# A two-block model step on one core: the end of the state-space branch and the last attention written in another order

## The reference

```python
def mamba2_branch(z, xbc, dt_raw, ...):
    xbc = silu(causal_dwconv(xbc, conv_w) + conv_b)
    xs, bm, cm = split(xbc)                       # 2048, 512, 512 channels
    dt = softplus(dt_raw + dt_bias)               # 32 heads of 64 channels, 4 groups
    y = ssd_chunked(xs, dt, -exp(a_log), bm, cm)  # per head: (cb * decay) @ (dt * x)
    y = y + d_skip[:, None] * xs                  # the D term
    yg = y * silu(z)                              # then a norm over each group of 512 channels
    yg = yg * rsqrt(mean(yg * yg, axis=-1, keepdims=True) + EPS)
    return (yg * norm_g) @ w_out

def sliding_window_attention(q, k, v, sinks):     # 12 query heads of 64, 2 key heads
    s = einsum(q, k) * 64 ** -0.5                 # masked to the band
    m = maximum(max(s), sink)
    p = exp(s - m); p = p / (sum(p) + exp(sink - m))
    return einsum(p, v)                           # rotary positions are applied to q and k before
```

## Time and profile before

| | us |
|---|---|
| median of 3 runs | 1700.3 (1697.75 to 1701.42) |
| profiled execution, own time | 1702.51 |
| its span | 1700.7 |
| z stage, transposes and cb, gate_b | 405.9 to 481.5 |
| y groups between mem_k and mem_v | 497.6 to 566.9 |
| group norm sums to the start of ssm_out | 566.9 to 588.4 |
| ssm_out, mix | 588.4 to about 660 |
| last attention, then wo1 | 1414.8 to 1474.3, from 1474.3 |

### The profile page before, as it was taken

How to read it: one execution, slowest core, us unless ns; L and a number is a source line. 1 busy time by engine, 2 the same in 40 slices (tenths; PEclk the granted TensorE clock), 3 DMA queues, 4 the chain that set the end, 5 groups by cost and what they waited for, 6 DMA issues and landing times.

```text
span 1700.7 us, 21777 instructions
## 1 busy us (share of the span) xinstructions
PE 1584.5 (93%) x8746; PEld 1357.5 (80%) x8746; DVE 583.1 (34%) x1040; ACT 807.3 (47%) x1192; POOL 1166.0 (69%) x490
## 2 busy tenths in 40 slices
PE   4999999999978698999999999889999988899997
PEld 3888879999967577878878888877888876578886
DVE  4111018245449712331121586552113046521100
ACT  4444363466353435355454773135444353355443
POOL 4888868887756286478877872606887952078883
PEclk9999999999989898999999998989999987899998
DMA  6555645555545154355545542004555631055551
GB/s 210 173 192 192 204 167 185 187 184 194 164 140 175 54 178 137 102 198 183 189 161 193 192 155 78 1 25 136 195 176 198 195 123 55 25 174 182 189 197 51
DMA packets 71861, 259.80 MB, mean 153 GB/s; under 512 B 7984, under 2 KB 8784, under 8 KB 71504
## 3 DMA queue, kind: packets, MB, share of 16 engines
q1 hardware_dynamic: 68832, 249.59, 44.3%
q10 hardware_dynamic: 2928, 8.81, 1.5%
HBM read 257.29 MB, written 1.08 MB: 152 GB/s over the span
## 4 chain that ended last, share of the span: by engine, by line
PE 86%; DVE 7%; ACT 5%; issue 2%; DMA 0%; POOL 0%; ACTq 0%; DVEq 0%
PE bank L459 12%; PE bank L461 12%; PE bank L460 12%; PE bank L429 7%; PE bank L430 7%; PE bank L431 6%; PE bank L488 5%; PE bank L490 5%; PE bank L489 5%; PE bank L568 1%; ACT w_hi L1000 1%; PE bank L614 1%; PE bank L840 1%; PE bank L852 1%; PE bank L637 1%
## 5 line engine op out<-in xcount | busy, mean ns | idle before, releaser
L387 POOL TENSOR_TENSOR w_lo<-raw,w_hi 128x1024 fp32r<-128x1024 f32 x474 | 1143.1, 2433 | 464.6 <-ACT w_hi L1000 464.1
L1000 ACT ACTIVATE w_hi<-raw 128x1024 fp32r<-128x1024 f32 x474 | 489.1, 1057 | 467.1 <-PE bank L461 211.6
L459 PE MATMUL bank<-w_hi,u_hi 128*128 128x512 f32 x880 | 352.1, 400 | 31.5 <-POOL w_lo L387 20.0
L461 PE MATMUL bank<-w_hi,u_lo 128*128 128x512 f32 x880 | 346.2, 393 | 0.0
L460 PE MATMUL bank<-w_lo,u_hi 128*128 128x512 f32 x880 | 346.1, 393 | 0.0
L429 PE MATMUL bank<-u_hi,w_hi 128*128 128x256 f32 x880 | 252.8, 287 | 12.9 <-DVE u_lo L1584 6.4
L430 PE MATMUL bank<-u_lo,w_hi 128*128 128x256 f32 x880 | 250.6, 285 | 0.0
L431 PE MATMUL bank<-u_hi,w_lo 128*128 128x256 f32 x880 | 250.6, 285 | 0.0
L459 PEld LDWEIGHTS bank<-w_hi,u_hi 128*128 128x128 f32 x880 | 167.4, 190 | 68.3 <-issue 22.7
L461 PEld LDWEIGHTS bank<-w_hi,u_lo 128*128 128x128 f32 x880 | 167.3, 190 | 36.0
L460 PEld LDWEIGHTS bank<-w_lo,u_hi 128*128 128x128 f32 x880 | 167.6, 190 | 33.4
(11 more groups left out here) (354 smaller groups left out, 1871.3 us busy)
## 6 DMA issues: line engine op xcount, KB each, us to landing
raw<-in_w SPq DMA_DIRECT2D x474, 512.0 KB, 4.2
bc<-acs_scratch ACTq DMA_DIRECT2D x8, 512.0 KB, 5.8
mem_t<-in_mem ACTq DMA_DIRECT2D x2, 1024.0 KB, 7.7
xf<-in_x ACTq DMA_DIRECT2D x2, 512.0 KB, 8.3
out<-out_t SPq DMA_DIRECT2D x4, 256.0 KB, 2.8
lvl<-in_lvl ACTq DMA_DIRECT2D x1, 448.0 KB, 5.6
band<-in_band ACTq DMA_DIRECT2D x1, 256.0 KB, 5.2
tri<-in_tri ACTq DMA_DIRECT2D x1, 192.0 KB, 7.8
```

Of the source, the lines that this page charges most:

```text
L387: nc.gpsimd.tensor_tensor(w_lo[:, q % RAW, :], raw[:, q % RAW, :], w_hi[:, q % HI, :].bitcast(F32), ALU.subtract).then_inc(split_done, 1)
L459: mm(b[:], hi[:, kt, a], w_hi[:, q % HI:q % HI + 2, c], start=kt == 0, stop=False)
L461: m = mm(b[:], lo[:, kt, a], w_hi[:, q % HI:q % HI + 2, c], start=False, stop=kt == KT - 1)
L1000: fn(w_hi[:, q % HI, :], raw[:, q % RAW, :], ACT.Copy).then_inc(hi_made, 1)
```

## The change

The state-space end is written anew, and so is the last attention; the start is changed a little.

- **dt first.** dt is ahead of xbc; its chain of small steps lies beside the convolution's taps (shares 1, 1, 3, 3, 4 of its steps beside the first five chunks), as do cols and the transposes of x behind chunks 6 to 10.
- **z and y tokens-first.** z is a pair stage. y has the decay tile stationary (128x128) and moves 64 columns of x; the D term is added on TensorE by four matmuls with the identity, of x that VectorE has scaled. Three `dec` buffers instead of two. After gating, the square with a sum along the row (ScalarE), root, reciprocal and scaling make the group norm; the matmuls with ones go. Then y is transposed (`y_turn`), and y_hi, y_lo are made from PSUM with the norm's weights.
- **Order of TensorE** from z on: z, with y groups 0 to 4 between its halves, gate_b with y groups 5 to 7, ssm_out, mem_k, mix, mem_v; the memory norm's squares, root and scaling lie under ssm_out; the merged turns and xattn's turns stand between mem_k and mem_v.
- **Last attention** ("merge and padding"): mq1 first, q1's halves between the heads, wo1's first tiles between the last heads; k, v and the memory's k, v in zero-padded tiles so that every matmul has 128 rows and 128 columns; rotation as two accumulated matmuls; 128 instead of 256 keys for the first query half; normalising on ScalarE; two heads accumulate into one output.
- **Start.** ScalarE and VectorE wait for `par` alone and no longer for ident, ones and tri; ScalarE feeds the first two pieces behind four u_hi steps.

```diff
-    ("xbc", 12, "row"), ("dt", 1, "row"), ("z", 8, "row"), ("gate_b", 4, "pair"),
-    ("mem_k", 4, "row"), ("mem_v", 4, "pair"), ("ssm_out", 8, "acc"), ("mix", 4, "proj"),
+    ("dt", 1, "row"), ("xbc", 12, "row"), ("z", 8, "pair"), ("gate_b", 4, "pair"),
+    ("ssm_out", 8, "acc"), ("mem_k", 4, "row"), ("mix", 4, "proj"), ("mem_v", 4, "pair"),
...
+            def y_heads(hg):
...
+                pe.wait_ge(W["decay"], hg + 1)
+                pe.wait_ge(W["x_d"], hg + 1)
+                for hh in range(4):
...
+                    mm(b0, d[:, hh, 0:P], x_dt[:, g, 0, o], start=first, stop=False, skip_group_check=True)
+                    mm(b1, d[:, hh, P:S], x_dt[:, g, 0, o], start=first, stop=False, skip_group_check=True)
+                    mm(b1, d[:, hh, S:384], x_dt[:, g, 1, o], start=False, stop=False, skip_group_check=True)
+                for t in range(2):
+                    for c in range(2):
...
+                        m = mm(flat(y_bank(g, c))[:, o], xbc[:, 2 * hg + t, c * P:c * P + P], ident[:], start=False,
+                               stop=hg % 2 == 1 and t == 1, skip_group_check=True)
+                m.then_inc(W["y_mm"], 1)
+            def y_turn(g):
+
+                for c in range(2):
+                    pe.wait_ge(W["g_n"], 2 * g + c + 1)
+                    for t in range(4):
+                        m = nc.tensor.transpose(quads(y_bank(g, c))[:, t, :], z[:, c, 512 * g + P * t:512 * g + P * t + P], ident[:])
+                    m.then_inc(W["y_t"], 1)
...
-            for g in range(4):
-                b = start_unit(U0["gn"] + g)
-                pe.wait_ge(W["g_sq"], g + 1)
-                for t in range(4):
-                    m = mm(b[:, 0, :], ones[:], sqg[:, t, :], start=t == 0, stop=t == 3)
...
+            y_heads(0)
+            half("z", 2, 0)
+            y_heads(1)
+            half("z", 2, 1)
+            y_heads(2)
+            y_turn(0)
+            half("z", 3, 0)
+            y_heads(3)
+            half("z", 3, 1)
+            y_heads(4)
+            y_turn(1)
+            half("gate_b", 0, 0)
+            y_heads(5)
+            half("gate_b", 0, 1)
+            y_heads(6)
+            y_turn(2)
+            half("gate_b", 1, 0)
+            y_heads(7)
+            half("gate_b", 1, 1)
+            y_turn(3)
...
+            acc_stage("ssm_out", lambda q: pe.wait_ge(W["y_lo"], 2 * (q // 4) + 2), None, lambda: merged_turn(0),
+                      (8, lambda: mem_sum(0, sq_mem, bank[(G0["mem_k"] + 3) % 4])), 4)
+            row_stage("mem_k", mm_hi, mm_lo, lambda kt: pe.wait_ge(mem_lo, kt // 2 + 1), sub=(0, 1))
+            merged_turn(1)
...
+            after(q0 + 9)
+            after(q0 + 11)
+            evict("z", 2, z, ACT.Silu)
+            decays(3)
+            y_square(0)
+            after(q0 + 13)
+            decays(4)
+            y_hi(0)
...
+                dve.wait_ge(W["seg_exp"], hg + 1)
+                v.tensor_tensor(dec[hg % 3][:], dec[hg % 3][:], cbm[:, hg // 2:hg // 2 + 1, :].to_broadcast([P, 4, 384]), ALU.mult).then_inc(W["decay"], 1)
...
+                if hg >= 2 and hg % 2 == 0:
+                    y_gate(hg // 2 - 1)
+                if hg + 2 < NHG:
+                    seg(hg + 2)
+                if hg >= 3 and hg % 2:
+                    y_norm(hg // 2 - 1)
...
+            row_stage("mq1", u_hi, u_lo)
+            rotate(0)
+            row_stage("q1", u_hi, u_lo, sub=(0, 1))
+            scores(0)
+            scores(1)
+            scores(2)
+            row_stage("q1", u_hi, u_lo, sub=(1, 1), halves=(0,))
+            rotate(1)
+            turns(0)
...
-            act.wait_ge(W["loaded_par"], 64)
+            act.wait_ge(W["loaded_par"], 16)
...
-                if kt in (1, 3):
-                    feed(1 if kt == 1 else 2)
+                if kt == 3:
+                    feed(2)
```

More of the change, by code:

```diff
@@ L969, in _ @@
-            pe.wait_ge(unit_free, _u)
-            proj_stage("wo1", u_hi, u_lo, lambda s, kt: None, lambda: turn("ffn3", 0))
+            rotate(0)
[6 more added lines that the diff above has]
+            turns(0)
+            row_stage("q1", u_hi, u_lo, sub=(1, 1), halves=(1,))
+            turns(1)
+            turns(2)
+            row_stage("q1", u_hi, u_lo, sub=(2, 1), halves=(0,))
@@ new lines, in _ @@
+            rotate(2)
+            heads_out(0)
+            turns(3)
+            turns(4)
+            heads_out(1)
+            row_stage("q1", u_hi, u_lo, sub=(2, 1), halves=(1,))
+            turns(5)
+            turns(6)
+            rotate(3)
+            heads_out(2)
+            turns(7)
+            turns(8)
+            heads_out(3)
+            turns(9)
+            turns(10)
+            heads_out(4)
+            pe.wait_ge(row_free, G0["q1"] + 3)
+            wo1_tiles(6, 7)
+            turns(11)
@@ L971, in _ @@
+            wo1_tiles(0)
+            turns(12)
+            heads_out(5)
+            wo1_tiles(1)
+            turns(13)
+            wo1_tiles(2)
+            turns(14)
+            heads_out(6)
+            wo1_tiles(3)
+            turns(15)
+            heads_out(7)
+            wo1_tiles(4, 5)
+            proj_stage("wo1", h_hi, h_lo, None, lambda: turn("ffn3", 0), pairs=(1,))
             ffn(3, lambda s: turn("ffn3", 1) if s == 0 else None, split_ready("ffn3"))
@@ new lines, in _, with evict @@
+            after(P0["dt"] - 1)
+            act.wait_ge(row_free, G0["dt"] + 1)
+            chain(act, W["row_step"], ROW_STEPS, "alog", lambda: fn(rows[5][0:32, 0:1], col("a_log", 0, 0, 32), ACT.Exp))
+            conv("xbc", "ssm_conv", "ssm_conv_b", xbc, 4, 12, beside)
+            def evict(name, p, dst, what):
+                for s in range(2):
+                    if s:
+                        act.wait_ge(piece_done, P0[name] + 4 * p + 4)
+                    else:
+                        act.wait_ge(s0_done, S0[name] + p + 1)
+                    fn(dst[:, s, 512 * p:512 * p + 512], flat(bank[(G0[name] + 2 * p + s) % 4]), what).then_inc(row_free, 1)
@@ new lines, in _ @@
+            decays(7)
+            y_square(2)
+            after(q0 + 21)
+            y_hi(2)
+            act.wait_ge(W["y_mm"], 8)
+            load(mem_t[:], mem_in, "loaded_mem")
+            y_square(3)
+            after(q0 + 23)
+            evict("gate_b", 1, sgb, ACT.Sigmoid)
+            y_hi(3)
+            q0 = P0["ssm_out"]
+            after(q0 + 2)
+            mem_squares(0, sq_mem)
+            after(q0 + 8)
+            mem_root(0, rs, bank[(G0["mem_k"] + 3) % 4])
+            after(q0 + 10)
@@ L1788, in merge @@
+            y_lo(2)
+            y_gate(3)
+            y_norm(3)
+            y_lo(3)
+            mem_norm(0, "mem_norm", sq_mem, rs, mm_hi, mm_lo)
+            dve.wait_ge(row_free, G0["mem_k"])
             def merge(s, d):
@@ L2082, in _ @@
+            rope(0)
             dve.wait_ge(W["loaded_band"], 32)
```

677 lines of the change are left out of this document (413 added, 264 removed).

## The result

The kernel after takes 1682.0 us (median of 4 runs, 1677.7 to 1682.9), before 1700.8; the ratio is 0.9888, with a 95% interval from 0.9867 to 0.9909. That is 19.0 us off, where 12.4 were forecast, inside the range. The profiled execution of after took 1677.70 us (span 1675.9), the fastest of its four, so the difference of the two traces (24.8 us) is some 6 us more than that of the medians.

The account below looks back on a forecast made before the run. TensorE, busy 93% of the span, was taken to bound the kernel. State-space end +1, last attention -10.4 and start -3 sum to -12.4 us on 1700.3, so 1688 us, range 1676 to 1703.

Parts of the forecast that it names:

- What bounds, and the waits removed: TensorE, busy 93% of the span, bounds the kernel; its seven waits around the state-space end go, -35.4 us.
- TensorE's work in the y phase: State-space end: a y group takes 3.7 us at 0.115 an instruction, y +17.4 us; with the other work +8.9.
- the lower bound of 0.058: y groups: us per 64-column f32 instruction if time halves with the columns; a group then takes 2.3, y +6.5 us.
- Rival 2: y phase: y is cheap at 0.058 us a narrow instruction and waits small; 1681 us, or 1675; chance 0.17.
- Waits added: State-space end: new TensorE waits, mainly 7.6, 6.6 and 5.9 us at three turns of y; +28.4 us together.
- Rival 1: y turns: slow VectorE steps beside GpSimd make seg 6 to 8 us, turn waits 13; 1706 us; chance 0.18.
- The slow clock behind the waits: State-space end: half clock behind each of three new large gaps, +9 us; old slow clock removed, -10 us.
- State-space end, sum: State-space end: work 8.9, waits removed -35.4, old slow clock -10, waits added 28.4, new slow clock 9; +1 us.
- Last attention: Last attention: 49.1 us against 59.5, -10.4, with 9 us of idle time left and ScalarE just under TensorE's pace.
- Rival 3: Last attention: ScalarE at 2.4 us a head sets the pace; -3 instead of -10.4, 1695 to 1697 us; chance 0.16.
- Rival 4: New y phase: ScalarE's table loads cost more than their row, 8 us for six in turn chains; 1696 us; chance 0.04.
- Start: Kernel start: TensorE starts 0.8 us earlier, the first norm some 2 us; -3 us (0 to -5).

Follow-up runs that it names:

- e4: Kernel after with ScalarE's squares and root of y's norm ahead of the next z eviction and exp, VectorE's scaling ahead of the decay product: 0.9755, 1658 us.
- e7: Kernel after with squares and root of y's norm ahead of the next z eviction and exp on ScalarE, VectorE's order unchanged: 0.9909, 3.6 us slower than after.
- e2: Kernel after with y's norm scaling ahead of the eight seg steps on VectorE instead of behind them: 0.9879, 1.5 us faster than after.
- e3: Kernel after with y_turn(0), (1) and (2) one half stage of weights later on TensorE: 0.9858, 5 us faster than after.
- a1: Kernel before with the new last attention alone, start and state-space end as before: 0.9917, 14.1 us faster than before.
- e1: Kernel after with the start of before (its waits and feeding of pieces): 0.9911, 1684.9 us.
- a4: Kernel after with the last attention's scores from only the head's own 64 rows of the padded tiles: 0.9982, 1697 us, 16 us slower than after.
- a2: Kernel after with wo1's first tiles behind all heads instead of between the last heads: 0.9934, 8 us slower than after.
- a3: Kernel after with the normalising of the last attention's probabilities back on VectorE: 0.9858, 5 us faster than after.

## Why the prediction was right, and where it was off

*What bounds, and the waits removed.* Right: all seven waits of the earlier trace rows are gone, and none came back at its place. The mergers wait 0.2 us for the memory norm under ssm_out, where I had set 1 and feared 10 or more.

*TensorE's work in the y phase.* A group takes 3.49 us instead of 3.7; the value taken from the nearest row was right, the lower bound of 0.058 was not. Rival 2 needed that bound and falls.

*Waits added.* The list of after's waits above has 21.6 + 3.8 + 1.7 + 1.4 + 0.2; with 0.6 at the cols turn that is 29.3 us, against 28.4 forecast, and the chain was right link by link. But the order of e4 shows that I read the chain as given: it was one of two ways to write the same streams, and e7 and e2 show that both queues have to be changed. Rival 1's condition (a seg of 6 to 8 us ahead of a turn) did not come about at the turns. Slow steps of seg(1) came ahead of the first y group, where GpSimd was at work: TensorE waits there 3.8 us in after's trace, 6.1 to 8.3 in the traces of e2, e3, e4 and e7. I had put 1.1 there.

*The slow clock behind the waits.* +9 forecast for three stretches; it is 12.3 in four. The first of them lies behind the wait at the first y group, which I had small.

*State-space end, sum.* +1 forecast; -1 by the runs, within what they can tell. Part of that is luck. a1 and e1 differ by the state-space part alone. By their traces TensorE's busy time rises by 4.3 us although 4.3 us less are lost to the clock in this phase, so its work rises by 8.6, as forecast (8.9). But its idle time falls by 3.5 us (115.6 to 112.1), where the forecast has 7.0 (28.4 - 35.4), and the loss to the clock (half of 30.96 and of 22.41 busy us at half clock) falls by 4.3, where the forecast has 1. Two misses of 3 us each cancel.

*Last attention.* This is the term that was mis-sized: -10.4 forecast, -14.1 measured. The sum ended at 1474.3, with the attention. The clock that before's heads had brought down stayed down into wo1 (28.3 us at 0.89, 3.1 us lost), and that came back too. And the reasons were only half mine: I gave the gain to overlapped weights and fewer keys, left 9.5 us of idle time nearly as it was, which was right, and priced the changes between 64 and 128 rows at nothing; a4 shows that the rows alone decide over 16 us, some 7 of them in the changes and the rest in the clock. That more than the whole gain of the part hangs on a piece to which the sum gave no price makes the nearness of the forecast partly luck. Rival 3 (the part gains 3 us) falls by a1, though its reason is half true. ScalarE at 2.4 us a head was "just under" TensorE's pace in my text; a2 and a3 show that it was over it, for 5 us in a3.

*Table loads.* Rival 4 falls: in the chain above, the load at 457.12 takes 1.28 us and the eviction starts at 458.42, as the load at 459.52 is followed by the exp at 460.81. The Trainium skill's drain of 1.38 us behind a load ("ScalarE: Activation LUTs", section "What ACT_TABLE_LOAD costs") shows in none of them, and the measurement decides.

*Start.* -3 forecast, -3.9 measured, by the mechanism named.

What stays open: how the 16 us of a4 divide in an execution other than the profiled one, and why the clock in e3 falls as long as in after with shorter gaps. Neither was tried by itself.

## What to carry to other kernels

When one result needs two engines' queues, look at both orders before moving the consumer: a piece that is ready early pays only if it stands early in every queue it passes (e4 against e2, e7 and e3). Gaps and changes of tile shape on TensorE can cost twice, once themselves and once through the clock that falls behind them and can stay down in the next stage, so a part's worth has to be read to the end of the stage after it. The other way round, taking away idle time that lies in a slow stretch gives less than its length if the clock stays down (e3).

## What the runs showed of the hardware

- A change between matmuls of 128 and 64 rows cost TensorE 0.10 to 0.22 us each in a4; four in a window head took 0.62 us, while twelve matmuls of 64 rows in a row were faster than twelve of 128 (1.92 and 2.40 us). The granted clock of the part was 0.88 in a4 and 0.98 in after.
- An f32 instruction with a 128x128 stationary tile takes 0.11 us with 64 moving columns and with 128 (both in after's y group): the halving saves nothing.
- VectorE's seg steps (128x128, within SBUF) take 0.27 us where GpSimd stands still and up to 2.5 us where it runs. TensorE's wait for the product behind seg(1) was between 3.8 and 8.3 us in kernels whose VectorE code up to there is the same; in after four of the steps ahead of that product were slow, in e7 six.
